# Multiplying the softmax rows by their inverse sums on POOL, in place of a product of ones with diagonal matrices

## The reference

```python
def attend_block(args):
    blk, qn, qr = args
    s = (jnp.einsum('bqhd,bkhd->bhqk', qn, k_nope, preferred_element_type=jnp.float32)
         + jnp.einsum('bqhr,bkr->bhqk', qr, k_rope, preferred_element_type=jnp.float32)) * SM_SCALE
    q_pos = blk * Q_BLOCK + jnp.arange(Q_BLOCK)
    s = jnp.where(key_pos[None, :] <= q_pos[:, None], s, NEG_INF)
    p = jax.nn.softmax(s, axis=-1).astype(v.dtype)
    return jnp.einsum('bhqk,bkhd->bqhd', p, v)
```

## Time and profile before

| | us |
|---|---|
| median of 3 runs | 3531.77 (3522.04 to 3534.57) |
| the profiled execution, its own time | 3531.3 |
| span of that execution in the profile | 3529.5 |
| PE busy | 3303.1 (94%) |
| DVE busy | 1671.8 (47%) |
| POOL busy | 1179.5 (33%) |
| ACT busy | 872.6 (25%) |
| one head of the latent attention, start to start | 47.98 |

### The profile page before, as it was taken

How to read it: one execution, slowest core, us unless ns; L and a number is a source line. 1 busy time by engine, 2 the same in 40 slices (tenths; PEclk the granted TensorE clock), 3 DMA queues, 4 the chain that set the end, 5 groups by cost and what they waited for, 6 DMA issues and landing times. The chain is left out here.

```text
span 3529.5 us, 51753 instructions
## 1 busy us (share of the span) xinstructions
PE 3303.1 (94%) x20484; PEld 2909.1 (82%) x20484; DVE 1671.8 (47%) x3164; ACT 872.6 (25%) x1675; POOL 1179.5 (33%) x739
## 2 busy tenths in 40 slices
PE   8999999988989999999999996689999999999997
PEld 7898989888978789888888885678888988888885
DVE  4646464634778332633333337335553533333335
ACT  3545454512122210311111114123331311111111
POOL 5434243410268234533333324010113633333323
PEclk9999999979999999999999998889999999999998
DMA  6111111140101212111111110000001111111111
GB/s 191 60 47 48 48 48 47 77 145 28 46 8 22 60 48 84 48 48 48 48 48 48 48 39 22 0 23 15 15 7 60 60 60 48 48 48 48 48 36 48
DMA packets 179280, 173.37 MB, mean 49 GB/s; under 512 B 50266, under 2 KB 162330, under 8 KB 178970
## 3 DMA queue, kind: packets, MB, share of 16 engines
q1 hardware_dynamic: 177566, 170.70, 15.3%
q10 hardware_dynamic: 1568, 0.61, 0.1%
HBM read 157.30 MB, written 19.23 MB: 50 GB/s over the span
## 5 line engine op out<-in xcount | busy, mean ns | idle before, releaser
L2186 DVE TENSOR_TENSOR x<-x,banks 128x512 f32<-128x512 f32 x512 | 344.5, 685 | 215.4 <-PE banks L80 215.4
L78 PE MATMUL banks<-winbuf_hi,xt_hi 128*128 128x256 f32 x1024 | 302.0, 295 | 12.1 <-ACT qkn L906 7.5
L80 PE MATMUL banks<-winbuf_hi,xt_lo 128*128 128x256 f32 x1024 | 290.2, 283 | 0.0
L79 PE MATMUL banks<-winbuf_lo,xt_hi 128*128 128x256 f32 x1024 | 290.2, 283 | 0.0
L78 PEld LDWEIGHTS banks<-winbuf_hi,xt_hi 128*128 128x128 f32 x1024 | 196.4, 192 | 31.3 <-ACT qkn L906 11.5
L78 PE MATMUL banks<-f2w_buf_hi,f2a_hi 128*128 128x512 f32 x512 | 200.9, 392 | 8.9 <-DVE x L2186 6.0
L78 PE MATMUL banks<-f1w_buf_hi,f1a_hi 128*128 128x512 f32 x512 | 201.3, 393 | 2.8 <-DVE f1a_lo L2179 2.8
L78 PE MATMUL banks<-h3t_hi,f2w_buf_hi 128*128 128x512 f32 x512 | 199.4, 390 | 1.6 <-issue 1.6
L78 PE MATMUL banks<-h1t_hi,f1w_buf_hi 128*128 128x512 f32 x512 | 199.4, 390 | 1.6 <-issue 1.6
L80 PE MATMUL banks<-f2w_buf_hi,f2a_lo 128*128 128x512 f32 x512 | 200.7, 392 | 0.0
L79 PE MATMUL banks<-f2w_buf_lo,f2a_hi 128*128 128x512 f32 x512 | 200.6, 392 | 0.0
(11 more groups left out here) (420 smaller groups left out, 8823.8 us busy)
## 6 DMA issues: line engine op xcount, KB each, us to landing
f1w_raw<-in_w_ff SPq DMA_DIRECT2D x32, 1024.0 KB, 5.1
f2w_raw<-in_w_ff SPq DMA_DIRECT2D x32, 1024.0 KB, 5.2
winraw<-in_w_in SPq DMA_DIRECT2D x128, 128.0 KB, 3.3
gluw_raw<-in_ssm_w_glu SPq DMA_DIRECT2D x16, 512.0 KB, 4.4
x<-in_x SPq DMA_DIRECT2D x8, 512.0 KB, 6.3
wow_raw<-in_w_out SPq DMA_DIRECT2D x4, 1024.0 KB, 5.3
x<-in_x SPq DMA_DIRECT2D x1, 4096.0 KB, 15.4
gew_raw<-in_w_ple_gate SPq DMA_DIRECT2D x4, 1024.0 KB, 5.2
```

Source lines behind the costliest of these rows:

```text
L78: nc.tensor.matmul(out, a.hi, b.hi, start=start, stop=False)
L79: nc.tensor.matmul(out, a.hi, b.lo, start=False, stop=False)
L80: return nc.tensor.matmul(out, a.lo, b.hi, start=False, stop=stop)
L2186: nc.vector.tensor_tensor(xx, xx, chip.ps[:, 4 + w % 4, :], ALU.add).then_inc(s_acc, 1)
```

## The change

DVE's `diag`, PE's ones product, and DVE's copy and multiplication into `prod` go. In their place POOL multiplies the exponentials `s` by the inverse sums while they still are rows, one query per partition, before PE transposes them (`normalise`). PE's transposes wait for POOL (`s_sm`) where they waited for ACT (`s_ex`), ACT and DVE read the PV result directly in PSUM (`value`), and DVE's reciprocal stands one tile earlier in its order. POOL's split for the next head, which stood at the start of a head, stands behind `normalise` of tile 4. The first `aow` split comes behind the last `normalise`.

```diff
@@ pool @@
+            def split(h, first):
                 pool.wait_ge(s_ld, h * 64 + 64)
-                pool.wait_ge(s_pj, h * 4 + 4)
-                pool.sem_inc(s_held, 1)
+                if not first:
+                    pool.wait_ge(s_pj, h * 4 + 4)
+                    pool.sem_inc(s_held, 1)
...
+            def normalise(h, t):
+                pool.wait_ge(s_r, h * NT + t + 1)
+                pool.sem_inc(s_held, 1)
+                w = (t + 1) * P
+                nc.gpsimd.tensor_scalar(s[:, t % 2, 0:w], s[:, t % 2, 0:w], z[:, t % 2:t % 2 + 1], None,
+                                        ALU.mult).then_inc(s_sm, 1)
+
+            split(0, True)
+            with pool.Fori(0, N_HEADS - 1) as h:
+                for t in range(NT):
+                    normalise(h, t)
+                    if t == 4:
+                        split(h + 1, False)
+            for t in range(NT):
+                normalise(N_HEADS - 1, t)
             then.do_split(pool, 0, 0)
@@ tensor @@
                 for t in range(NT):
-                    pe.wait_ge(s_ex, h * NT + t + 1)
+                    pe.wait_ge(s_sm, h * NT + t + 1)
...
                     if t >= 2:
-                        pe.wait_ge(s_pr, h * NT + (t + 7))
-
-                    pe.wait_ge(s_dg, h * NT + t + 1)
-                    pe.sem_inc(s_held, 1)
-                    nc.tensor.matmul(chip.ps[:, 6 + t % 2, P:2 * P], ones[:, :], diag[:, t % 2, :], start=True, stop=True)
+                        pe.wait_ge(s_ol, h * NT + (t + 7))
+                        pe.sem_inc(s_held, 1)
+
                     pe.wait_ge(s_ta, h * NT + t + 1)
                     pe.wait_ge(s_td, h * NT + t + 1)
@@ scalar @@
                 def expo(t):
                     w = (t + 1) * P
+                    if t >= 2:
+                        act.wait_ge(s_sm, h * NT + t - 1)
...
-                    act.wait_ge(s_pr, h * NT + (t + 9))
-                    nc.scalar.activation(token_rows(ot.hi, h, t), prod[:, t % 2, :].rearrange("p (c r) -> p c r", r=NT),
-                                         ACT.Copy).then_inc(s_oh, 1)
+                    act.wait_ge(s_o, h * NT + t + 1)
+                    nc.scalar.activation(token_rows(ot.hi, h, t), value(t), ACT.Copy).then_inc(s_oh, 1)
@@ vector @@
+                def inverse(t):
+                    dve.wait_ge(s_ex, h * NT + t + 1)
+                    nc.vector.reciprocal(z[:, t % 2:t % 2 + 1], z[:, t % 2:t % 2 + 1]).then_inc(s_r, 1)
...
                 maximum(1)
+                inverse(0)
                 for t in range(NT):
                     w = (t + 1) * P
-
-                    dve.wait_ge(s_ex, h * NT + t + 1)
-                    nc.vector.reciprocal(z[:, t % 2:t % 2 + 1], z[:, t % 2:t % 2 + 1]).then_inc(s_r, 1)
-                    dve.wait_ge(s_r, h * NT + t + 1)
-                    nc.vector.tensor_scalar(diag[:, t % 2, :], chip.ident[:, :], z[:, t % 2:t % 2 + 1], None,
-                                            ALU.mult).then_inc(s_dg, 1)
+                    if t + 1 < NT:
+                        inverse(t + 1)
...
-                    dve.wait_ge(s_o, h * NT + t + 1)
-                    nc.vector.tensor_copy(prod[:, t % 2, :], chip.ps[:, 6 + t % 2, P:2 * P]).then_inc(s_rc, 1)
-                    dve.wait_ge(s_rc, h * NT + t + 1)
-                    nc.vector.tensor_tensor(prod[:, t % 2, :], prod[:, t % 2, :], chip.ps[:, 6 + t % 2, 0:P],
-                                            ALU.mult).then_inc(s_pr, 1)
```

More of the change, by code:

```diff
@@ L2342, in stage_attention @@
     with ExitStack() as ctx:
-        (s_ld, s_hi, s_wsp, s_pj, s_ph, s_pl, s_pd, s_rk, s_qrt, s_qrh, s_qrl, s_sc, s_mx, s_nm, s_ex, s_r, s_dg,
-         s_t, s_ta, s_td, s_o, s_pr, s_oh, s_ol, s_mask, s_held, s_rc, s_fold) = sems(
-            nc, ctx, "at", "ld hi wsp pj ph pl pd rk qrt qrh qrl sc mx nm ex r dg t ta td o pr oh ol mask held rc fold")
+        (s_ld, s_hi, s_wsp, s_pj, s_ph, s_pl, s_pd, s_rk, s_qrt, s_qrh, s_qrl, s_sc, s_mx, s_nm, s_ex, s_r, s_sm,
+         s_t, s_ta, s_td, s_o, s_oh, s_ol, s_mask, s_held, s_fold) = sems(
+            nc, ctx, "at", "ld hi wsp pj ph pl pd rk qrt qrh qrl sc mx nm ex r sm t ta td o oh ol mask held fold")
         raw = [chip.at("kvw", 160, [P, KV, KW]), chip.at("qw", 162, [P, KQ, NOPE + P])]
@@ L2354, in stage_attention @@
         fold = chip.at("fold", 203.5, [P, P])
-        diag = chip.at("diag", 204, [P, 2, P])
-        prod = chip.at("prod", 205, [P, 2, VH])
-        ones = chip.at("ones", 206.5, [P, P])
         mx = chip.at("mx", 207.25, [P, 2])
@@ L2363, in stage_attention, with value @@
         block = ctx.enter_context(nc.Block())
+        def value(t):
+            return chip.ps[:, 6 + t % 2, 0:P].rearrange("p (c r) -> p c r", r=NT)
         @block.sync
@@ L2382, in _ @@
         def _(pool):
-            nc.gpsimd.memset(ones[:, :], 1.0).then_inc(s_mask, 1)
             nc.gpsimd.memset(mask[:, :], 0.0).then_inc(s_mask, 1)
-            pool.wait_ge(s_mask, 2)
+            pool.wait_ge(s_mask, 1)
             nc.gpsimd.affine_select(out=mask[:, :], in_=mask[:, :], compare_op=ALU.is_ge, fill=NEG,
                                     base=0, pattern=[[-1, P]], channel_multiplier=1).then_inc(s_mask, 1)
-            with pool.Fori(0, N_HEADS) as h:
+            def split(h, first):
                 pool.wait_ge(s_ld, h * 64 + 64)
-                pool.wait_ge(s_pj, h * 4 + 4)
-                pool.sem_inc(s_held, 1)
+                if not first:
+                    pool.wait_ge(s_pj, h * 4 + 4)
+                    pool.sem_inc(s_held, 1)
                 for n in range(2):
@@ L2402, in _ @@
             pe.sem_inc(s_pj, 4)
-            pe.sem_inc(s_pr, NT)
-            pe.wait_ge(s_mask, 3)
+            pe.sem_inc(s_ol, NT)
+            pe.wait_ge(s_mask, 2)
             pe.wait_ge(s_fold, 2)
@@ L2432, in _ @@
                 last.then_inc(s_pj, 1)
-                pe.wait_ge(s_pr, h * NT + NT)
+                pe.wait_ge(s_ol, h * NT + NT)
                 pe.sem_inc(s_held, 1)
@@ L2561, in low_part @@
                     hi, lo = (token_rows(o, h, t) for o in (ot.hi, ot.lo))
-                    nc.vector.tensor_tensor(lo, prod[:, t % 2, :].rearrange("p (c r) -> p c r", r=NT), f32(hi), ALU.subtract).then_inc(s_ol, 1)
+                    nc.vector.tensor_tensor(lo, value(t), f32(hi), ALU.subtract).then_inc(s_ol, 1)
+                def inverse(t):
+                    dve.wait_ge(s_ex, h * NT + t + 1)
+                    nc.vector.reciprocal(z[:, t % 2:t % 2 + 1], z[:, t % 2:t % 2 + 1]).then_inc(s_r, 1)
                 maximum(0)
                 maximum(1)
+                inverse(0)
                 for t in range(NT):
                     w = (t + 1) * P
-                    dve.wait_ge(s_ex, h * NT + t + 1)
-                    nc.vector.reciprocal(z[:, t % 2:t % 2 + 1], z[:, t % 2:t % 2 + 1]).then_inc(s_r, 1)
-                    dve.wait_ge(s_r, h * NT + t + 1)
-                    nc.vector.tensor_scalar(diag[:, t % 2, :], chip.ident[:, :], z[:, t % 2:t % 2 + 1], None,
-                                            ALU.mult).then_inc(s_dg, 1)
+                    if t + 1 < NT:
+                        inverse(t + 1)
                     dve.wait_ge(s_t, h * NT + t + 1)
```

## The result

The changed kernel takes 3584.47 us (median of 4 runs, 3582.54 to 3590.40) against 3526.90 of the kernel before beside it: a ratio of 1.0158, 95% interval 1.0135 to 1.0182, so some 57 us slower. The forecast was 3544, which is 12.8 us above the kernel before, with a range of 3533 to 3564: wrong. The result was nearest to the rival "slow POOL and the clock" (3569, chance 0.08).

The account below looks back on a forecast made before the run. PE, busy 94% of the span, was taken as the bound. Seven heads at +1.98, the last head's +0.32 and -1.36 for the diag stall gave +12.8 us on 3531.3: 3544 us, range 3533 to 3564.

Parts of the forecast that it names:

- slow POOL and the clock: Rival: dear POOL multiplication, and PE's clock falling in the 3.0 us gap before tile 5's transposes: 3569 us, chance 0.08.
- what is taken away: Ones products of tiles 2, 3 and 4 save 0.66 us a head; DVE's removed instructions save nothing, save 1.36 once.
- I take the second: POOL's multiplication priced by CAST's slope through the 128-column row: 0.44 + 0.86 per 1000 columns, 1.32 us at 1024.
- The third reading: Rival price from POOL's two TENSOR_SCALAR rows: 0.29 + 2.06 per 1000 columns, 2.40 us at 1024; 3558, chance 0.22.
- T(5): Tile 5's transposes on PE wait 1.66 us for POOL behind the split: start at offset 19.58, 1.98 later than before.
- Hidden, with 0.6 to spare: At tile 7, POOL's link lets the transposes start at 27.66, before PV(6) frees PE at 28.26: no wait.
- The tail: From tile 5's transposes to the next head: unchanged at 12.38 us, carrying the 1.98 us lateness to the head's end.
- `diag` stall: In the last head PE stood 1.36 us for DVE's diag; its removal gains 1.36 us, once.
- the slower case: POOL's first aow split after the last head: just hidden, but 0.5 us late if POOL is slower.
- The hidden case: Rival: split hidden and POOL as cheap as CAST, 3530; with tile 0's link free, 3523; hidden or gained, chance 0.08.
- The port: DVE's negation of the maximum meeting POOL's split: given nothing; blocking would put up to 1 us on a tile's chain.
- the two slow cases: Rivals with a dear POOL multiplication: 3558 without a clock fall, chance 0.22; 3569 with it, chance 0.08.

Follow-up runs that it names:

- no_multiply: Changed kernel without POOL's multiplication, its split right after the projections (output not the reference's): 3521.31 us, ratio 0.9965 to the kernel before.
- narrow: Changed kernel with POOL multiplying only the first 128 columns of each tile (output not the reference's): 3533.52 us, ratio 1.0005 to the kernel before.
- filler: Changed kernel with ten useless float32 matmuls of 128 columns on PE ahead of tile 5's transposes: 3572.99 us, ratio 1.0124 to the kernel before.
- dve_multiply: Changed kernel with the multiplication on DVE instead of POOL, POOL's split behind tile 5's multiplication: 3539.89 us, ratio 1.0014 to the kernel before.
- split_last: Changed kernel with POOL's split behind the multiplication of tile 7, not tile 4: 3561.01 us, ratio 1.0079 to the kernel before.
- narrow_last: narrow with POOL's split behind tile 7 instead of tile 4 (output not the reference's): 3537.28 us in a single execution.
- dve_split_end: Changed kernel with multiplication on DVE, POOL's split behind the last tile and awaited in halves: 3522.26 us, ratio 0.9966 to the kernel before.
- first_tile_first: dve_split_end with ACT copying v, and DVE serving tile 0's reciprocal and multiplication before tile 1's maximum: 3522.69 us, ratio 0.9979 to the kernel before.

## Why the prediction was wrong

Where the stage's +52.0 us come from, by the runs, each step by the difference of two stages:

| | us | forecast |
|---|---|---|
| what is taken away (before to no_multiply) | -8.12 | -6.6 |
| the link at 0.60 us a tile, split at 4 (no_multiply to narrow) | +13.95 | |
| POOL's price per column, its waits and the clock (narrow to after) | +46.16 | |
| the last two together | +60.11 | +19.4 |

Of the +46.16, some 12 are the clock: the 12.1 us by which the filler's seven heads are shorter.

**The step that failed** is the size of one term, "I take the second": POOL's TENSOR_SCALAR by the slope of CAST, 0.44 + 0.86 per 1000 columns. It measured 0.28 + 2.50: 0.60 us at 128 (forecast 0.55), 1.88 at 640 (0.99), 2.20 at 768 (1.10), 2.84 at 1024 (1.32). The third reading, 2.06 by the two rows of the operation itself, was the nearest and still too low. It had been set aside since one of its rows was 128x1. A short row and a long one of the same operation were better evidence than the slope of another operation.

The Trainium skill, "GPSIMD Engine Reference", section "Engine selection", calls one-input operations on GpSimd "roughly line-rate"; the measurement agrees for CAST (0.86 ns a column) and disagrees for this TENSOR_SCALAR (2.50).

**The mechanism held.** With the measured prices the prediction's own sum for T(5) gives 12.25 + 0.45 + 1.88 + 4.64 + 2.20 + 0.15 = 21.57; with the 0.47 us that T(2) waits, 22.04; measured 22.14. T(0) was forecast at 3.50 and came at 3.60, the split takes as long as before, and T(5) waits for POOL, only in heads with a split.

**What grew out of the price** makes up the head's 5.0 us above the forecast: 0.1 at T(0); about 0.5 at T(2), where 128x384 is no longer done in time; 1.9 at T(5); and 2.4 behind it. Of these, 1.6 are the clock (filler) and 0.74 the wait at T(7), which the text called "Hidden, with 0.6 to spare". The rival priced the clock at 1.5 us a head, and rightly made it depend on a gap of about 3 us; its T(7) wait, 0.48, was also near. It fell short since its slope was 2.06 and it had no wait at T(2).

**The tail** was to carry the lateness unchanged, 12.38 us. It grew to 14.81. That is the clock and T(7) again: with the fillers' 1.57 and the 0.74 off, 12.50.

**The last head** was forecast 1.04 us shorter with its `diag` stall. It was 1.9 longer, while the seven heads before it are 49.9 longer together (the one of 56.22 among them): no split, but POOL's price at each tile, and `aow` late by 0.7, where the slower case had 0.5 (2.73 us of waiting where the earlier trace rows has 2.05):

```profile
2742.95 1.06 PE L2479 MATMUL banks<-ident,s 128*128 128x128 f32 x8 [0.74 <-POOL s L2403]
...
2749.59 0.55 PE L78 MATMUL banks<-aow_buf_hi,ot_hi 128*128 128x256 f32 x1 [2.73 <-PEq L2342]
```

**What is taken away** was right in kind: 0.75 us a head against 0.66, and not 1.76 for all eight products, with the `diag` stall on top. The hidden case of the rivals priced the same thing at 0.88 a head, for which the prediction gives no working; 0.75 lies between the two.

**The port** was rightly given nothing in this change, since the negation of the maximum is one column wide. It became real as soon as DVE took the multiplication (dve_multiply): that of tile 6 took 1.34 us more, where the prediction had said "up to 1 us", and 0.74 of it reached the head's length.

**The clock.** That no fall follows a gap of 1.66 us was nearly right for a gap of that size: the wait of 1.78 us at T(0) was followed by a fall in 4 of 40 heads (eight each of the changed kernel, split_last, narrow, narrow_last and filler). It was the gap that was wrong, 2.70 us, and behind it the clock fell in 7 heads of 7.

**The chances.** 0.22 and 0.08 for the two slow cases were too little, given that the only two rows of the operation spoke for them. The upper end, 3564, cut off the case that came nearest.

## What to carry to other kernels

Price an operation by rows of that operation at two widths, even where one is tiny, before you borrow the slope of another; where nothing else is there, put the dearer reading first if its engine becomes a link of a chain on which PE waits. An engine that was idle two thirds of the time is not free for a link: what is queued on it between two links (here 4.64 us of splitting) adds to the chain, and PE pays what its own work does not cover: 0.6 us a head with a link of 0.60 us, 3.6 with the real one. The same edit with the multiplication on DVE and the split behind the last tile gained what the removal promised, less the first tile's link.

## What the runs showed of the hardware

- POOL's TENSOR_SCALAR by a column of scalars costs 2.50 ns a column, three times its CAST (0.86) and more than its two-input TENSOR_TENSOR (1.81 us for 768 columns, 2.36 ns a column with the fixed part in it). DVE does it at 0.51.
- A DVE TENSOR_SCALAR of 128x896 that meets a POOL instruction took 2.02 us for 0.68. POOL's own duration did not change (1.84 and 1.81 us).
- A gap of 2.70 us in PE's work was followed by a granted clock of 0.66 over 5 us, and cost 1.57 us more than its own length. With 2.4 us of useless matmuls in it the clock stayed at 1.00 and the stage was 8.4 us shorter. Shorter gaps were followed by a fall less often: 2.30 us in 4 heads of 7 (dve_multiply), 1.78 in 4 of 40. These are counts of this kernel; no run looks for a limit.
- The code ahead of the stage is the same in all kernels, yet takes from 2301.8 (dve_split_end) to 2318.2 us (no_multiply) in the profiled executions, in which different stretches run at 1.2 GHz. That is more than most effects told here, so small ones were read in the stage.
- The whole time follows the clock as well. dve_split_end is 12 us faster by its ratio (interval 7 to 17) and only 3.05 by its stage. Its twelve executions had a mean granted clock of 0.9733, the 29 of the kernel before beside them 0.9708. An estimate of the time at full clock is each execution's time multiplied by its granted clock; the mean of that is 3.1 us lower (interval 1 to 5), as in the stage. Likewise no_multiply comes out 8.3 us faster (stage 8.1), narrow 5.4 slower (5.8) where its ratio shows nothing, and split_last 26.0 slower (26.5). first_tile_first comes out 7.1 us faster (5.0). So what the ratio of dve_split_end has beyond its stage is the clock of the rest of the program, where no line was changed; whether the edit or chance shifted it, no run settles.
